# Two feed-forward layers of a two-block network: sixteen of 22 gate/up tile pairs as seven block products

## The reference

```python
for l in range(DEPTH):                       # DEPTH = 2
    ...
    h = rms_norm(x, g_ffn[l])
    x = x + (jax.nn.silu(h @ w1[l]) * (h @ w3[l])) @ w2[l]
```

## Time and profile before

| | us |
|---|---|
| median of 3 runs | 3241.65 |
| span of the profiled execution | 3241.1 |
| TensorE busy | 3216.7 (99%) |
| VectorE, ScalarE, GpSimd busy | 1801.7, 1305.7, 631.9 |
| weight chunks loaded | 529, 512 KB each, 3.3 from issue to landing |
| chain of waits: share of TensorE | 87% |

### The profile page before, as it was taken

One profiled execution on the slowest core, in us unless ns is written; L12 is line 12 of the kernel. 1 busy time (PEld: TensorE's weight loads), 2 busy tenths in 40 slices (PEclk: granted clock), 3 DMA queues, 4 the chain that ended last, 5 costly groups with the idle time before them and its releaser, 6 DMA issues.

```text
span 3241.1 us, 38219 instructions
## 1 busy us (share of the span) xinstructions
PE 3216.7 (99%) x15436; PEld 2689.0 (83%) x15436; DVE 1801.7 (56%) x2728; ACT 1305.7 (40%) x1991; POOL 631.9 (19%) x502
## 2 busy tenths in 40 slices
PE   9999999999999999999999999999999999999998
PEld 7888888888888888888888888888888898788887
DVE  6865775444348655845443465554544268974433
ACT  5653553333237534633322323332323248743221
POOL 1521241111005311520110022111111013521101
PEclk9999999999999999999999999999999999999999
DMA  4122323323221122332233222222223322223332
GB/s 137 48 74 68 108 89 104 101 98 102 93 93 59 60 78 87 109 94 94 95 101 103 96 81 81 82 91 92 93 97 97 99 85 93 93 92 100 97 98 85
DMA packets 85136, 295.60 MB, mean 91 GB/s; under 512 B 9568, under 2 KB 12128, under 8 KB 84960
## 3 DMA queue, kind: packets, MB, share of 16 engines
q1 hardware_dynamic: 84384, 292.76, 27.4%
q10 hardware_dynamic: 576, 0.40, 0.0%
HBM read 291.02 MB, written 2.10 MB: 90 GB/s over the span
## 4 chain that ended last, share of the span: by engine, by line
PE 87%; DVE 7%; ACT 3%; issue 1%; POOL 1%; DMA 1%; SPq 0%; ACTq 0%; DVEq 0%; POOLq 0%
PE bank L313 86%; PE bank L316 2%; DVE wl L569 2%; ACT m_p L536 1%; DVE small L1304 1%; DMA raw<-in_wts 1%; ACT wh L533 1%; POOL u_g L591 1%; DVE u_uc L565 0%; DVE m_ptl L569 0%; DVE c_kl L569 0%; DVE m_qf L559 0%; ACT m_pth L533 0%; DVE u_t L565 0%; DVE m_sh L809 0%
## 5 line engine op out<-in xcount | busy, mean ns | idle before, releaser
L569 DVE TENSOR_TENSOR wl<-raw,wh 128x1024 fp32r<-128x1024 f32 (+1 forms) x531 | 661.1, 1248 | 760.7 <-ACT wh L533 759.8
L313 PE MATMUL bank<-zh,wh 128*128 128x512 f32 (+1 forms) x2652 | 1025.0, 386 | 6.1 <-ACT zh L533 6.1
L313 PE MATMUL bank<-zh,wl 128*128 128x512 f32 (+1 forms) x2652 | 1019.9, 385 | 1.9 <-DVE wl L569 1.9
L313 PE MATMUL bank<-zl,wh 128*128 128x512 f32 (+1 forms) x2652 | 1018.3, 384 | 2.2 <-DVE zl L572 2.1
L533 ACT ACTIVATE wh<-raw 128x1024 fp32r<-128x1024 f32 (+1 forms) x531 | 555.8, 1052 | 534.8 <-PE bank L313 468.6
L313 PEld LDWEIGHTS bank<-zh,wl 128*128 128x128 f32 x2652 | 498.6, 188 | 107.4 <-DVE wl L569 7.2
L313 PEld LDWEIGHTS bank<-zh,wh 128*128 128x128 f32 x2652 | 499.0, 188 | 102.3 <-ACT zh L533 6.1
L313 PEld LDWEIGHTS bank<-zl,wh 128*128 128x128 f32 x2652 | 499.0, 188 | 98.6 <-DVE zl L572 3.7
L313 PE MATMUL bank<-f_mh,wh 128*128 128x512 f32 (+1 forms) x748 | 285.2, 381 | 0.0
L313 PE MATMUL bank<-f_mh,wl 128*128 128x512 f32 (+1 forms) x748 | 283.3, 379 | 0.0
L313 PE MATMUL bank<-f_ml,wh 128*128 128x512 f32 (+1 forms) x748 | 280.8, 375 | 0.0
(11 more groups left out here) (337 smaller groups left out, 4471.2 us busy)
## 6 DMA issues: line engine op xcount, KB each, us to landing
raw<-in_wts SPq DMA_DIRECT2D x529, 512.0 KB, 3.3
c_nb<-in_c_bias SPq DMA_DIRECT2D x16, 384.0 KB, 3.2
x<-in_xT SPq DMA_DIRECT2D x8, 256.0 KB, 5.9
out<-x SPq DMA_DIRECT2D x13, 128.0 KB, 1.8
b_mask<-in_b_mask SPq DMA_DIRECT2D x2, 576.0 KB, 4.4
r_d<-in_decay SPq DMA_DIRECT2D x4, 256.0 KB, 2.7
raw<-in_wts SPq DMA_DIRECT2D x2, 256.0 KB, 3.7
m_t<-in_mla_tab SPq DMA_DIRECT2D x2, 256.0 KB, 4.8
```

The costliest lines, as they stand in the source:

```text
L313: return self.e.matmul(out, l, r, start=start, stop=stop, skip_group_check=inside)
L569: return self.e.tensor_tensor(out, src, b32(hi), ALU.subtract)
```

## The change

The 22 pairs are done in two parts of 11, each followed by its own part of the w2 product: eight tiles of 11 steps, added to x, then the same for the second part. Matmuls with w2 stay 528.

Pairs are of three kinds. U (0 to 3) are as before. N (4, 5) and S (6 to 21) read activations already multiplied by 1/rms (`n_x`, split into `nh`, `nl`), for which VectorE computes 8 products once per layer.

An S unit treats gate and up tile as a 2 x 2 block product: the 1024 rows are two halves of 4 tiles, the tokens two halves of 256. Eight block products (4 tiles x 3 passes x 256 columns each) become seven of Strassen-Winograd form: P1, P2, P3, Q4, P5, P6, P7. For that four activation sums (`th`, `tl`, 1024 columns each) are made once per layer; they overwrite z after pair 3. Per unit there are four weight sums: S1 covers two of them (1024 columns, VectorE), S2 one (512, VectorE), S4 one (512, GpSimd). The unit's weights arrive as two loads a and b in a pair of raw slots; there are two such pairs now. Its ring chunks are part 0 (8 tiles: P1, P6), part 2 (P7, P5), part 3 (4 tiles: P2) and part 1 (Q4, P3); part 1 of unit i is run behind part 0 of unit i + 1 (`tail`). S1 and S2 are computed by VectorE ahead of the low half of the chunk before part 0. Slot a is freed by S4, slot b by the low half of part 1. The results are put together on ScalarE (s1, g1) and VectorE (s2, s3, u7, g2, u6), 256 columns each. The table loads of `sync_mix` wait for the first output tile of the second w2 part. The core of the diff:

```diff
+HALF = 11
+KINDS = "UUUUNNSSSSS" + "SSSSSSSSSSS"
...
+    def load(self, sem="wl"):
+        n, slot = len(self.book.plan), self.slot
+        self.slot = (slot + 1) % self.slots
+        self.book.plan.append([])
+        self.book.loads.append((slot, self.held.get(slot, self.first)))
+        self.held[slot] = sem, "rel", n
+        return n
...
+    def product(self, w, side, x, k0, out, fresh, *event):
+        for k in range(4):
+            cs = slice(512 * side + 128 * k, 512 * side + 128 * k + 128)
+            xh, xl = x(k0 + k)
+            self.wait_ge("wh", *w[3])
+            self.mm(out, w[1][:, cs], xh, fresh and k == 0, False, True)
+            self.mm(out, w[1][:, cs], xl, False, False, True)
+            self.wait_ge("wl", *w[3])
+            t = self.mm(out, w[2][:, cs], xh, False, k == 3, True)
+        t.then_inc(*self.tell("mm", event, *self.spent(w)))
...
+    def high_s(self, c, part, unit, a, b):
+        m, wh = self.m, self.m.wh[c % RING]
+        src = m.s_raw[self.book.loads[a][0] // 2]
+        if part == 0:
+            self.wait_ge("wl", "S2", *unit)
+            self.cp(wh, src[:, 0:1024]).then_inc(*self.tell("wh", c))
+        elif part == 1:
+            self.wait_ge("pl", "S4", *unit)
+            self.cp(wh, src[:, 1024:2048]).then_inc(*self.tell("wh", c))
+        elif part == 2:
+            self.wait_ge("wl", "S1", *unit)
+            self.cp(wh, m.s_b).then_inc(*self.tell("wh", c))
+        else:
+            landed(self, b)
+            self.cp(wh[:, 0:512], src[:, 1536:2048]).then_inc(*self.tell("wh", c))
...
     def split(self, c):
+        after = self.book.s_next(c)
+        if after:
+            self.sums(*after[2:])
...
+    def sums(self, unit, a, b):
+        src = m.s_raw[self.book.loads[a][0] // 2]
+        landed(self, a)
+        landed(self, b)
+        if self.free_b:
+            self.wait_ge("wl", *self.free_b)
+        self.tt(m.s_b, src[:, 0:1024], src[:, 512:1536], ALU.add).then_inc(*self.tell("wl", "S1", *unit))
+        self.wait_ge("wl", "S1", *unit)
+        self.tt(src[:, 512:1024], m.s_b[:, 512:1024], src[:, 0:512], ALU.add).then_inc(*self.tell("wl", "S2", *unit))
+    def low_s(self, c, part, unit, a, b):
+        m, wh, wl = self.m, self.m.wh[c % RING], self.m.wl[c % RING]
+        src = m.s_raw[self.book.loads[a][0] // 2]
+        self.wait_ge("wh", c)
+        if part == 0:
+            self.lo(wl, src[:, 0:1024], wh).then_inc(*self.tell("wl", c))
+        elif part == 1:
+            self.lo(wl, src[:, 1024:2048], wh).then_inc(*self.tell("wl", (c,), ("rel", b)))
+        elif part == 2:
+            self.lo(wl, m.s_b, wh).then_inc(*self.tell("wl", c))
+            self.free_b = (c,)
+        else:
+            self.lo(wl[:, 0:512], src[:, 1536:2048], wh[:, 0:512]).then_inc(*self.tell("wl", c))
...
+def tensor_unit(L, F, l, i, tail):
+    m = L.m
+    unit = F + (i,)
+    at = slice(128 * i, 128 * i + 128)
+    loads = L.s_loads()
+    tile = lambda w, k: (("w1", "w3")[w], (l,), 128 * k, range(128 * i, 128 * i + 128))
+    L.book.plan[loads[0]] += [tile(w, k) for w in range(2) for k in range(4)]
+    L.book.plan[loads[1]] += [tile(w, k) for w in (1, 0) for k in range(4, 8)]
+    w = L.s_chunk(0, unit, loads)
+    A, B, C, D = unit_banks(i)
+    a = L.claim(A, "cp", "g1", *unit)[:, 0:256]
+    L.product(w, 0, normed_quarter(L, F, 0), 0, a, True, "P1", *unit)
+    b = L.claim(B, "ev", "s2", *unit)[:, 0:256]
+    L.product(w, 1, token_sum(L, F, 1), 0, b, True, "P6", *unit)
+    tail()
+    w = L.s_chunk(2, unit, loads)
+    c = L.claim(C, "ev", "u6", *unit)[:, 0:256]
+    L.product(w, 0, token_sum(L, F, 2), 0, c, True, "P7", *unit)
+    d = L.claim(D, "ev", "g2", *unit)[:, 0:256]
+    L.product(w, 1, token_sum(L, F, 0), 0, d, True, "P5", *unit)
+    w = L.s_chunk(3, unit, loads)
+    L.wait_ge("cp", "s1", *unit)
+    L.product(w, 0, normed_quarter(L, F, 0), 4, a, False, "P2", *unit)
+    def last():
+        w = L.s_chunk(1, unit, loads)
+        L.wait_ge("ev", "s3", *unit)
+        L.product(w, 0, token_sum(L, F, 3), 0, c, False, "Q4", *unit)
+        L.wait_ge("ev", "u7", *unit)
+        L.product(w, 1, normed_quarter(L, F, 1), 4, d, False, "P3", *unit)
+    return last
...
 def tensor_ffn1(L, l):
     F, N, nxt = ("f", l), ("ffn", l), after_ffn1(l)
     quad = [F + (w, i) for i in range(2) for w in range(2)]
     L.group(quad, 8, L.z(*N), w13_desc, range(4), [("ev",) + n for n in quad], {3: L.stat(N), 5: L.spread(N)})
-    for i in range(2, FF):
-        n = [F + (w, i) for w in range(2)]
-        L.group(n, 8, L.z_whole(), w13_desc, [f_bank(i, w) for w in range(2)], [("ev",) + x for x in n])
-    for i in range(0, 8, 2):
-        n = [("w2", l, i), ("w2", l, i + 1)]
-        L.group(n, FF, mids_of(L, F), w2_desc, [w2_bank(i), w2_bank(i + 1)], [("xx",) + nxt + (i + j,) for j in range(2)])
+    tensor_units(L, F, l, range(2, HALF))
+    for j in range(0, 8, 2):
+        n = [("w2a", l, j), ("w2a", l, j + 1)]
+        L.group(n, HALF, half_mids(L, F, 0), w2_half(0), [w2a_bank(j), w2a_bank(j + 1)],
+                [("xx", "half", l, j + i) for i in range(2)])
+    tensor_units(L, F, l, range(HALF, FF))
+    L.use_slots(RAWS)
+    for j in range(0, 8, 2):
+        n = [("w2", l, j), ("w2", l, j + 1)]
+        L.group(n, HALF, half_mids(L, F, 1), w2_half(1), [w2_bank(j), w2_bank(j + 1)],
+                [("xx",) + nxt + (j + i,) for i in range(2)])
...
+def vector_token_sums(L, F):
+    m = L.m
+    (xa, xb), (ta, tb) = m.n_x, m.n_t
+    L.wait_ge("ev", "n", *F, 7)
+    L.tt(by_tile(ta), quarter(xa, 0), quarter(xa, 1), ALU.subtract).then_inc(*L.tell("ev", "t", *F, 0))
+    L.tt(by_tile(tb), quarter(xb, 1), quarter(xa, 1), ALU.subtract).then_inc(*L.tell("ev", "t", *F, 2))
+def vector_token_sum(L, F, j):
+    m = L.m
+    xb, (ta, tb) = m.n_x[1], m.n_t
+    L.wait_ge("hi", "t", *F, j)
+    L.lo(m.tl[j], (ta, ta, tb, tb)[j], m.th[j]).then_inc(*L.tell("lo", "t", *F, j))
+    if j == 0:
+        L.wait_ge("lo", "t", *F, 0)
+        L.tt(by_tile(ta), by_tile(ta), quarter(xb, 1), ALU.add).then_inc(*L.tell("ev", "t", *F, 1))
+    if j == 2:
+        L.wait_ge("lo", "t", *F, 2)
+        L.wait_ge("ev", "t", *F, 1)
+        L.tt(by_tile(tb), by_tile(ta), quarter(xb, 0), ALU.subtract).then_inc(*L.tell("ev", "t", *F, 3))
+def vector_s3(L, F, i):
+    m = L.m
+    s1, s2, s3 = s_of(m, i)
+    a, t, b, mf = m.f_t[i % 2]
+    c, d = (m.bank[n][:, 0:256] for n in unit_banks(i)[2:])
+    L.wait_ge("mm", "P7", *F, i)
+    L.wait_ge("ev", "s2", *F, i)
+    if KINDS[i - 2] == "S":
+        L.wait_ge("ev", "u7", *F, i - 2)
+    L.tt(s3, c, s2, ALU.add).then_inc(*L.tell("ev", "s3", *F, i))
+    L.wait_ge("mm", "P5", *F, i)
+    L.wait_ge("ev", "s3", *F, i)
+    if KINDS[i - 2] != "N":
+        L.wait_ge("pl", *F, i - 2)
+    L.tt(half(b, 1), d, s3, ALU.add).then_inc(*L.tell("ev", "u7", *F, i))
+def vector_unit_out(L, F, i):
+    m = L.m
+    s1, s2, s3 = s_of(m, i)
+    a, t, b, mf = m.f_t[i % 2]
+    c, d = (m.bank[n][:, 0:256] for n in unit_banks(i)[2:])
+    L.wait_ge("mm", "P3", *F, i)
+    if KINDS[i - 2] != "N":
+        L.wait_ge("ev", "u", *F, i - 2)
+    L.tt(half(a, 1), d, s2, ALU.add).then_inc(*L.tell("ev", "g2", *F, i))
+    L.wait_ge("mm", "Q4", *F, i)
+    L.tt(half(b, 0), c, s2, ALU.add).then_inc(*L.tell("ev", "u6", *F, i))
...
+def gpsimd_s4(L, F, i):
+    unit = F + (i,)
+    c = L.book.s_at(3, unit)
+    a, b = L.book.ring[c][3:]
+    src = L.m.s_raw[L.book.loads[a][0] // 2]
+    L.wait_ge("wl", "S2", *unit)
+    L.wait_ge("wl", c)
+    L.tt(src[:, 1536:2048], src[:, 512:1024], src[:, 1536:2048], ALU.add).then_inc(
+        *L.tell("pl", ("S4",) + unit, ("rel", a)))
+def scalar_units(L, F, l, units):
+    for i in (*units, None):
+        prev = units[-1] if i is None else i - 1
+        first = i == units[0] and i > 0 and i == HALF
+        if i is not None and KINDS[i] == "S":
+            scalar_s1(L, F, i)
+        if not first and KINDS[prev] == "S":
+            scalar_unit_gate(L, F, prev)
+        if not first:
+            scalar_half_mid(L, F, l, prev)
+        if i is not None and KINDS[i] == "N":
+            scalar_unit_gate(L, F, i)
+        if i is not None and KINDS[i] == "S":
+            scalar_g1(L, F, i)
+        L.ahead()
+def vector_units(L, F, units):
+    for i in (*units, None):
+        prev = units[-1] if i is None else i - 1
+        first = i == units[0] and i == HALF
+        if i is not None and KINDS[i] == "S":
+            vector_s2(L, F, i)
+        if not first and KINDS[prev] == "S":
+            vector_unit_out(L, F, prev)
+            vector_unit_gate(L, F, prev)
+        if i is not None and KINDS[i] == "S":
+            vector_s3(L, F, i)
+        if not first:
+            vector_half_mid(L, F, prev)
+        if i is not None and KINDS[i] == "N":
+            vector_unit_gate(L, F, i)
+        L.ahead()
...
 def scalar_ffn1(L, l):
-    m, nxt = L.m, after_ffn1(l)
+    m, nxt, F = L.m, after_ffn1(l), ("f", l)
```

(72 more changed lines are left out.)

235 lines of the change are left out of this document (214 added, 21 removed).

## The result

The change makes the kernel slower: 3368.2 us (median of 4 runs, 3366.3 to 3371.2) against 3241.6 (3241.4 to 3242.4), ratio 1.0389, 95% interval 1.0375 to 1.0404. The forecast was 3342, its range 3275 to 3395, its likeliest case's own range 3320 to 3375. The profiled execution took 3368.8 us, its span 3367.1; so 1.7 us lie outside a span, not the 0.55 that the forecast allowed.

What follows compares the result with a forecast made beforehand. The prediction took matmul time to bound the kernel while other engines keep up; S stages limited by a queue loop add 82.0 us and the units before them 18.6: 3241.1 + 82.0 + 18.6 = 3341.7, so 3342 us, range 3275 to 3395.

Steps and rivals of the forecast that it cites:

- likeliest case: Whole kernel: the queue loop sets the S units' time and the edges add some; 3342 us, chance 0.60.
- The matmuls of an S unit are cheaper: TensorE in an S unit: 84 matmuls take 9.90 us, 0.98 less than a pair; 31.4 us over both layers.
- VectorE's order, not its busy time, sets a turn: S-unit loop: 8.70 us of VectorE work, but queue order and a load make each turn 14.65 us.
- GpSimd's sum holds the gate product: S-unit loop: the fourth weight sum on GpSimd delays VectorE's gate product, which ends at 4.46 us; 0.31 us of the loop.
- stall behind the quad: Before the S units: added VectorE work makes the seventh chunk's low half late, 5.4 us a layer.
- token sums: Before unit 5: the four sums wait for the last plain unit and delay the next unsplit chunk, 3.9 us a layer.
- five S units: First run of S units in a layer: start, two loop turns and end take 63.6 us.
- eleven: Second run of S units in a layer: start, eight loop turns and end take 151.5 us.
- The end of a run: From the last unit's part 0 to the end of its last product: 5.5 + 6.1 + 2.6, 14.2 us.
- the clock falls: Rival, chance 0.06: pauses drop TensorE to 1.2 GHz, its matmuls set the unit's pace at 19.8 us; 3445 us.
- The third unit of the first run: Start of a run of S units: the third unit's part 0 is ready 20.07 us after the first matmul.
- splits run ahead and TensorE keeps the pace: Rival, chance 0.12: S units take TensorE's 9.90 us, under 10.3, with part 0 split before the mid; 3220 us.

Runs made afterwards that it cites:

- e2: The changed kernel with a third pair of raw weight slots (six in place of four): 3331.7 us, 36.5 faster than the change's 3368.2.
- the reordered kernel: The e6 kernel with VectorE's list of an S unit reordered and the last part 1 split before the mid: 3227.6 us, ratio 0.9959 to the kernel before.
- e9: The reordered kernel with one more chunk split, on both engines, ahead of the normed copies in units 0 to 2: 3231.6 us, ratio 0.9965.
- e12: The e9 kernel with the extra chunk split only in units 0 and 1, no longer in unit 2: 3230.2 us, ratio 0.9967.
- e6: Changed kernel with third slot pair, part 0 split before mid, GpSimd's two operations on VectorE; then normed copies spread, token sums reordered, one chunk between: 3249.1 us.
- e3: The changed kernel with ScalarE's high half of next part 0 ahead of the mid's copy, two slot pairs as before: 3328.7 us, 39.5 faster.
- e8: The changed kernel with 26 unused 256-column matmuls ahead of each part 0 but a run's first, and of the last part 1: 3370.3 us.

## Why the prediction was right, and where its sizes were off

Confirmed in kind, with what was measured:
- The matmuls of an S unit are cheaper: 0.86 us for the forecast's 0.98 where they run without a pause, 27.5 for 31.4 in all. (The row of 67 starts gave 0.1178 a matmul; in the units it is 0.1193.)
- VectorE's order, not its busy time, sets a turn: 14.61 for 14.65, with both waits where they were put, 3.00 and then 0.24 to 1.82 us. Each was taken away alone and together, and the turn followed. That it agrees to 0.04 us is in part luck: one turn differs from the next by up to 0.2.
- GpSimd's sum holds the gate product: the gate product lasts 0.89 for 0.69 and ends at 851.60 (forecast 4.46 behind the sum, measured 4.47). The Trainium skill (SBUF — State Buffer, "Who interferes with whom") calls the port that the two engines share an exclusive lock; these rows agree.
- The down parts and the late table loads cost nothing: the two feed-forwards are 62.1 and 64.0 us longer (from the quad's last chunk to the end of the down product), which is all of the 126.1 between the spans.

Two of the signs did not come: TensorE is idle for 2.67 us in the turn shown, not 4 to 5, and the stall behind the quad is 7.35 us, not 3 to 6.

Mis-sized. By landmark (first matmul of each stage; for the stalls the stage's time less its matmuls at 0.2267), layer 0, forecast and measured in us: stall behind the quad 5.4 and 7.35; token sums 3.9 and 3.25; five S units 63.6 and 70.2; eleven 151.5 and 155.5. That is 11.9 more than forecast in this layer; the next has 13.5 by the same landmarks; together 25.4 of the 26 between 3342 and 3368.

*The end of a run* ("from the last unit's part 0 to the end of its last product"), forecast 14.2 us, is 18.2 and 18.1 in layer 0 and 18.5 and 19.0 in layer 1: 17.0 of the 25.4. This is the term that was most mis-sized. TensorE, VectorE, then TensorE again:

```profile
914.26 0.58 PE L358 MATMUL bank<-n_h,wl 128*128 128x256 f32 x1 [0.76 <-DVE wl L675]
914.64 0.42 PE L358 MATMUL bank<-n_h,wh 128*128 128x256 f32 x1
914.86 0.41 PE L358 MATMUL bank<-n_l,wh 128*128 128x256 f32 x1
```
```profile
921.52 0.76 DVE L665 TENSOR_TENSOR f_t<-bank,s_s 128x256 f32<-128x256 f32 x2 [1.45 <-PE bank L358]
...
926.34 1.22 DVE L675 TENSOR_TENSOR wl<-s_raw,wh 128x1024 fp32r<-128x1024 f32 x1 [3.00 <-ACT wh L616]
```
```profile
927.96 0.58 PE L358 MATMUL bank<-zh,wh 128*128 128x256 f32 x1 [2.17 <-DVE s_s L665]
928.34 0.41 PE L358 MATMUL bank<-zl,wh 128*128 128x256 f32 x1
928.55 0.42 PE L358 MATMUL bank<-zh,wl 128*128 128x256 f32 x1
```

VectorE's g2 starts 7.3 us behind the last part 0, forecast 5.5: the first matmuls between begin 0.21 us apart, not 0.12; the granted clock had fallen behind the pauses (1.6 of the + 1.8). The chain from there to the end of part 1's split is as forecast (6.04 for 6.1). Then 0.4 for the combination s3, which I left out, and 4.4 us of matmuls for 2.6, most at half clock again (+1.8, of which 0.2 is that they are 24 and I had counted 22). So the rival "the clock falls" was right in its event and wrong in its price. Only some 16 of a unit's 84 matmuls, those behind the pauses, are slow (856.25 to 859.45), and inside the loop they fill TensorE's idle time (pauses of 1.9 and 0.76 us where I had 3.5 and 1); at the ends there is no idle time to fill. That holds for this kernel: with the load out of the loop (e2) the same fall costs 0.86 us a turn.

*The third unit of the first run* has its part 0 at 22.5 us, forecast 20.07 (20.5 in the second run; 21.4 and 20.3 in layer 1). The low half of part 1, which frees the slot, ends 9.2 us behind the run's first matmul (655.43), forecast 8.0: a split beside GpSimd's sum lasted 1.93 us, and the evacuations of the plain unit before stand ahead. The load then took 4.49 us to land for 3.3.

*The stall behind the quad.* I took GpSimd's product at 1.29 us. Its second one met two long VectorE operations:

```profile
604.14 3.31 POOL L733 TENSOR_TENSOR f_t<-f_t 128x512 f32<-128x512 f32 x1 [4.48 <-DVE f_t L671]
```
```profile
603.98 1.22 DVE L665 TENSOR_TENSOR n_ta<-n_xa 128x1024 f32<-128x1024 f32 x1
605.12 1.22 DVE L665 TENSOR_TENSOR n_tb<-n_xb,n_xa 128x1024 f32<-128x1024 f32 x1
609.10 2.36 DVE L675 TENSOR_TENSOR wl<-s_raw,wh 128x1024 fp32r<-128x1024 f32 x2 [2.76 <-ACT wh L616]
```

The product is locked out for the length of both, the mid's copy starts at 607.49, and with it all behind it is 2 us late: 7.35 for 5.4.

The rival "splits run ahead and TensorE keeps the pace", 3220, describes the reordered kernel: 3227.6. Its condition (a unit under 10.3 us, part 0 split before the mid) held there and in its variants e9 and e12 alone.

What stays open: the rest of the edges. The reordering of e6 took some 13 of their 22 us away; the last 9.6 were then only moved (0.1 and some 7.1 us a layer in e9, 3.2 and 4.0 in e12).

## What to carry to other kernels

Where a change adds work to a half-idle engine, step through one turn of its queue in program order, across the engines and the buffer that it frees, before trusting the busy sum: here 8.70 us of work took 14.6. When one wait of such a loop is opened, read the next turn anew: another wait takes its place (36.5 and 39.5 alone, 90.4 both), and a lower clock that cost nothing behind a longer wait can begin to cost (0.86 us a turn). And the two operations given to GpSimd to relieve VectorE were paid by VectorE, where both read two SBUF operands; taking them back brought 13 us (36.0 over the kernel before on its chip, then 22.6).

## What was not expected of the hardware

- GpSimd's 512-element product lasted 3.31 us in place of 1.29 when VectorE ran two 1024-element operations back to back: it did not get in between them.
- TensorE fell to its lower level (1.2 GHz) behind short pauses. In the reordered kernel, pauses of 1.22 and 0.60 us are followed by 512-column matmuls that begin 0.43 us apart (0.23 otherwise), for some 2.5 us:

```profile
616.61 0.47 PE L359 MATMUL bank<-n_h,wh 128*128 128x512 f32 x1 [1.22 <-ACT wh L617]
...
617.91 0.79 PE L359 MATMUL bank<-n_h,wl 128*128 128x512 f32 x1 [0.60 <-DVE wl L676]
...
618.93 0.63 PE L359 MATMUL bank<-n_l,wh 128*128 128x512 f32 x1
619.36 0.63 PE L359 MATMUL bank<-n_h,wl 128*128 128x512 f32 x1
```

- Pauses of much the same length did not always go with the same clock. In e3, with pauses of 0.5 to 0.76 us alone, three or four in a turn of some 13.4, the clock stayed at 1.00 (820 to 900 us). In e2 it stayed at 1.00 from 806 to 819 us with pauses of 1.38 and 0.76, fell behind the next 1.41 and 0.75, and then stayed at 0.87 with 0.74 and 0.76 in each turn of 13.54. These runs give no rule for it.
- A 512 KB load that lands in 3.1 to 3.5 us in most turns took 4.0 to 5.2 in some, for no reason that the traces show: every third in e3, one in each of three of e8's runs of S units.
